# Chunk inverses by doubling: new partition halves for the middle product, masks on the product, and key scores and values inside the loop

## What is computed

```
def step(S, inp):
    r_t, w_t, k_t, v_t, kk_t, b_t = inp
    sa = einsum('bhvk,bhk->bhv', S, -kk_t)
    S = S * w_t[:, :, None, :] + sa[..., None] * b_t[:, :, None, :] + v_t[..., None] * k_t[:, :, None, :]
    return S, einsum('bhvk,bhk->bhv', S, r_t)
```

## Time and profile before

| | us |
|---|---|
| three runs | 2098.78, 2099.97, 2102.54 |
| median | 2099.97 |
| the profiled execution's own time | 2097.59 |
| its span, first to last instruction | 2095.7 |
| PE busy | 2038.5 (97% of the span) |
| DVE busy | 1278.4 (61%) |
| ACT busy | 890.4 (42%) |
| POOL busy | 131.5 (6%) |

### The profile page before, as it was taken

How to read it: one execution, slowest core, us unless ns; L and a number is a source line. 1 busy time by engine, 2 the same in 40 slices (tenths; PEclk the granted TensorE clock), 3 DMA queues, 4 the chain that set the end, 5 groups by cost and what they waited for, 6 DMA issues and landing times.

```text
span 2095.7 us, 32549 instructions
## 1 busy us (share of the span) xinstructions
PE 2038.5 (97%) x12860; PEld 1642.9 (78%) x12860; DVE 1278.4 (61%) x1564; ACT 890.4 (42%) x1219; POOL 131.5 (6%) x162
## 2 busy tenths in 40 slices
PE   7999999999999999999999999999999999999999
PEld 6689778878668888978878678877856888897887
DVE  7785465557765545665667655567865554566553
ACT  4432244434534434444545444434423444434442
POOL 2210100000010001000002011000000000000000
PEclk9999999999999999999999999999999999999999
DMA  8410165546247564555555258553312655555554
GB/s 298 128 63 4 42 201 186 182 160 203 99 152 210 185 205 161 171 193 188 165 186 191 74 168 226 187 191 124 115 54 92 202 187 181 170 172 181 183 172 147
DMA packets 92520, 335.31 MB, mean 160 GB/s; under 512 B 11150, under 2 KB 11284, under 8 KB 92095
## 3 DMA queue, kind: packets, MB, share of 16 engines
q1 hardware_dynamic: 85536, 311.62, 45.0%
q0 software_dynamic: 6880, 22.16, 3.7%
HBM read 332.69 MB, written 1.05 MB: 159 GB/s over the span
## 4 chain that ended last, share of the span: by engine, by line
PE 88%; DVE 7%; POOL 2%; issue 1%; ACT 1%; DMA 0%; DVEq 0%; SPq 0%; ACTq 0%; POOLq 0%
PE acc L327 40%; PE acc L404 20%; PE acc L380 10%; PE acc L829 2%; DVE w_lo L1431 2%; PE acc L577 2%; PE aux L577 1%; PE aux L750 1%; PE aux L960 1%; PE aux L953 1%; PE aux L785 1%; POOL rstd L2185 1%; POOL stat L2188 1%; PE aux L817 1%; PE aux L424 1%
## 5 line engine op out<-in xcount | busy, mean ns | idle before, releaser
L1431 DVE TENSOR_TENSOR w_lo<-w_raw,w_hi 128x1024 fp32r<-128x1024 f32 x588 | 716.3, 1225 | 590.3 <-ACT w_hi L1078 585.7
L1078 ACT ACTIVATE w_hi<-w_raw 128x1024 fp32r<-128x1024 f32 x588 | 620.3, 1059 | 805.0 <-PE acc L327 457.4
L327 PE MATMUL acc<-w_hi,operand_hi 128*128 128x512 f32 x1344 | 533.9, 397 | 26.3 <-DVE operand_lo L1586 11.9
L327 PE MATMUL acc<-w_hi,operand_lo 128*128 128x512 f32 x1344 | 525.0, 391 | 0.0
L327 PE MATMUL acc<-w_lo,operand_hi 128*128 128x512 f32 x1344 | 524.4, 390 | 0.0
L327 PEld LDWEIGHTS acc<-w_hi,operand_hi 128*128 128x128 f32 x1344 | 253.0, 188 | 87.5 <-DVE operand_lo L1452 15.0
L327 PEld LDWEIGHTS acc<-w_hi,operand_lo 128*128 128x128 f32 x1344 | 252.8, 188 | 53.8
L327 PEld LDWEIGHTS acc<-w_lo,operand_hi 128*128 128x128 f32 x1344 | 253.2, 188 | 50.5 <-issue 0.5
L404 PE MATMUL acc<-w_hi,hidden_hi 128*128 128x512 f32 x528 | 210.1, 398 | 0.0
L404 PE MATMUL acc<-w_hi,hidden_lo 128*128 128x512 f32 x528 | 208.5, 395 | 0.0
L404 PE MATMUL acc<-w_lo,hidden_hi 128*128 128x512 f32 x528 | 208.5, 395 | 0.0
(11 more groups left out here) (403 smaller groups left out, 2090.1 us busy)
## 6 DMA issues: line engine op xcount, KB each, us to landing
w_raw<-in_weights SPq DMA_DIRECT2D x588, 512.0 KB, 3.4
ln_gain<-in_gains POOLq DMA_DIRECT2D x7, 512.0 KB, 5.0
bias_at<-in_rpb POOLq DMA_DIRECT2D x12, 256.0 KB, 5.6
ln_gain<-in_ln_g POOLq DMA_DIRECT2D x4, 512.0 KB, 4.1
ln_bias<-in_ln_b POOLq DMA_DIRECT2D x4, 512.0 KB, 5.9
vec_rw<-in_vec POOLq DMA_DIRECT2D x3, 512.0 KB, 7.4
l_rw<-in_lora SPq DMA_DIRECT2D x1, 1152.0 KB, 10.6
iclr_rw<-in_xT SPq DMA_DIRECT2D x2, 512.0 KB, 4.5
```

Of the source, the lines that this page charges most:

```text
L327: mm = pe.matmul(acc[:, 2 * pair + t, :], (ah, al)[x][:, kt, t * P:(t + 1) * P], W[w][:, s, kk * 512:(kk + 1) * 512], start=(kt == 0 and ( ...
L1078: act.activation(whi[:, s, :], raw[:, s, :], ACT.Copy).then_inc(w_hi[s], 1)
L1431: dve.tensor_tensor(wlo[:, s, :], raw[:, s, :], whi[:, s, :].bitcast(F32), ALU.subtract).then_inc(w_lo[s], 1)
```

## The change

It edits six places; the diff below is cut where lines only repeat a pattern.

1. `LOWN` and all that makes it goes: 16 matmuls on PE, one DVE operation, two semaphores.
2. `by_own_rows` is called four times instead of twice, two of them with the column half swapped. The swapped copy goes to bank 6 and 7 and feeds `INV` directly from PSUM (`set_inverse`), so that `INV` holds its matrices on the other partition half from `INVT`.
3. `product` writes its result to the other half; `extension` reads `INV` and `TM` there and interleaves its two products kt by kt, so that four matmuls in a row use the four combinations of row and column half.
4. The mask moves from the extensions to the product: DVE now copies the product under the mask into a `TM` that holds the identity (`masked_product`), ACT copies the two extensions unmasked, and POOL puts the identity back into `TM` after each extension (16 copies of 128x512), having set it once before the loop (2 copies of 128x1024).
5. The four `by_both_rows` calls on `KTT` move into the loop, after g = 0, 1, 3 and 5, all on banks 6 and 7, each waiting for DVE's `set_keys` of the one before; the gates come after g = 7 and 9, and `keys_by_values` is interleaved with products 14, 15, 18 and 19.
6. DVE's order changes: `masked_product(0)` and `(1)` stand between the `set_turned` calls; the four splits come after `set_inverse(1)`; the wait for the gains is in `biased(0)`; the two `centred` calls stand ahead of `masked_product(14)`.

```diff
-            for n in range(len(STEPS) - 1):
-                for s in range(2):
-                    of = half_of(s)
-                    mm = pe.matmul(aux[of, 3, n * CH:(n + 1) * CH], LOWT[of, n, :], ident[of, of], start=True, stop=True, skip_group_check=True)
-            mm.then_inc(m["low_ready"], 1)
...
-            by_own_rows(6, 1)
+            by_own_rows(6, 0, swapped=1)
             pe.wait_ge(m["n_copied"], due(m["n_copied"], 2))
-            by_both_rows(0, 1, 0, BTT)
+            by_own_rows(0, 1)
             pe.wait_ge(m["rb_copied"], due(m["rb_copied"]))
-            by_both_rows(2, 1, 1, BTT)
+            by_both_rows(2, 1, 0, BTT)
             pe.wait_ge(m["rb_copied"], due(m["rb_copied"]))
-            by_both_rows(4, 0, 0, KTT)
...
+            by_both_rows(4, 1, 1, BTT)
+            pe.wait_ge(m["inv_set"], due(m["inv_set"], 2))
+            by_own_rows(6, 1, swapped=1)
...
+            def product(g, with_values=None):
+                u, b = g % UNITS, g % 2
+                for kt in range(KT):
+                    for s in range(2):
+                        of = half_of(s)
+                        mm = pe.matmul(ps(b)[half_of(1 - s), kt * CH:(kt + 1) * CH], NM[of, u // 2, u % 2, kt, :], INVT[of, u // 2, u % 2, kt, :],
+                                       start=(kt == 0), stop=(kt == KT - 1), skip_group_check=True)
+                    if with_values is not None:
+                        keys_by_values(with_values, kt)
+                mm.then_inc(m["t_ready"], 1)
...
             def extension(g):
...
+                if g == 0:
+                    pe.wait_ge(m["rb_copied"], due(m["rb_copied"], 2))
+                elif g >= 2:
+                    pe.wait_ge(m["e_copied"], due(m["e_copied"], 2 if g - 2 < last * UNITS else 1))
+                b = 2 + u if n == last else 2 + 2 * (g % 2)
+                for kt in range(KT):
+                    cols = slice(kt * CH, (kt + 1) * CH)
+                    for s in range(2):
+                        mm = pe.matmul(ps(b)[half_of(s), cols], INV[half_of(1 - s), t, e, kt, :], TM[half_of(1 - s), t, e, kt, :],
+                                       start=(kt == 0), stop=(kt == KT - 1), skip_group_check=True)
+                    if n < last:
+                        for s in range(2):
+                            mm = pe.matmul(ps(b + 1)[half_of(1 - s), cols], TM[half_of(1 - s), t, e, kt, :], INV[half_of(1 - s), t, e, kt, :],
+                                           start=(kt == 0), stop=(kt == KT - 1), skip_group_check=True)
+                mm.then_inc(m["e_ready"], 1)
+
+            def keys(k):
+                if k == 0:
+                    pe.wait_ge(m["inv_set"], due(m["inv_set"], 2))
                 else:
+                    pe.wait_ge(m["akrk_copied"], due(m["akrk_copied"]))
+                by_both_rows(6, k // 2, k % 2, KTT)
...
+            between = {0: lambda: keys(0), 1: lambda: keys(1), 3: lambda: keys(2), 5: lambda: keys(3), 7: lambda: gate(0), 9: lambda: gate(1)}
+            values_in = {14: 0, 15: 1, 18: 2, 19: 3}
...
# ACT, inside the loop
-                act.wait_ge(m["t_ready"], due(m["t_ready"]))
-                act.activation(TM[:, u // 2, u % 2], heads_of(4 + g % 2), ACT.Copy).then_inc(m["t_copied"], 1)
...
+                act.wait_ge(m["e_ready"], due(m["e_ready"]))
+                act.activation(INVT[:, t, e], heads_of(b), ACT.Copy).then_inc(m["e_copied"], 1)
+                if n < last:
+                    act.activation(INV[:, t, e], heads_of(b + 1), ACT.Copy).then_inc(m["e_copied"], 1)
+                if g in (14, 18):
+                    rhs((g - 14) // 4)
...
# DVE
+            def masked_product(g):
+                n, u = g // UNITS, g % UNITS
+                if g == 0 or g >= UNITS:
+                    dve.wait_ge(m["t_reset"], due(m["t_reset"], 1 if g else TT))
+                dve.wait_ge(m["t_ready"], due(m["t_ready"]))
+                dve.copy_predicated(TM[:, u // 2, u % 2], many(LOWT[:, n, :].bitcast(U32), KT), heads_of(g % 2)).then_inc(m["t_copied"], 1)
...
+            set_turned(1, 0, 2)
+            masked_product(0)
+            set_turned(1, 1, 4)
+            masked_product(1)
             set_inverse(1)
-            set_keys(0, 0, 4)
-            set_keys(0, 1, 6)
-            set_keys(1, 0, 0)
-            set_keys(1, 1, 2)
...
             ahead(q + 20, 4)
-            between = {0: lambda: bonus(0), 1: lambda: bonus(1), 2: lambda: biased(0), 3: lambda: biased(1), 4: lambda: gated(0),
-                       5: means, 6: lambda: centred(0), 7: lambda: centred(1), 9: lambda: gated(1)}
...
+            between = {2: lambda: set_keys(0), 3: lambda: set_keys(1), 4: lambda: bonus(0), 5: lambda: set_keys(2), 6: lambda: bonus(1),
+                       7: lambda: set_keys(3), 8: lambda: biased(0), 9: lambda: gated(0), 10: lambda: biased(1), 11: lambda: gated(1), 12: means}
+            for g in range(2, UNITS * len(STEPS)):
+                if g == 14:
+                    centred(0)
+                    centred(1)
+                masked_product(g)
                 if g in between:
                     between[g]()
...
# POOL
+            pool.wait_ge(m["rows_turned"], due(m["rows_turned"], 8))
+            for t in range(TT):
+                pool.tensor_copy(TM[:, t].rearrange("p e k n -> p (e k) n"), I64[:].unsqueeze(1).to_broadcast([P, HEADS, CH]))\
+                    .then_inc(m["t_reset"], 1)
             for k, name in enumerate(("gn_g", "gn_b")):
                 load(GN[:, k, :], A[name].partition_broadcast(P), m["gn_in"])
+            for g in range(UNITS * (len(STEPS) - 1)):
+                u = g % UNITS
+                pool.wait_ge(m["e_ready"], due(m["e_ready"]))
+                pool.tensor_copy(TM[:, u // 2, u % 2], I64[:].unsqueeze(1).to_broadcast([P, KT, CH])).then_inc(m["t_reset"], 1)
```

More of the change, by code:

```diff
@@ L530, in freed, with by_own_rows @@
                 pe.wait_ge(m["rows_copied_v"], due(m["rows_copied_v"]))
-            def by_own_rows(b, t):
+            def by_own_rows(b, t, swapped=0):
                 for kt, e, s in each():
                     of, at = half_of(e), chunk(t, s)
-                    mm = pe.matmul(ps(b + e)[half_of(s), kt * CH:(kt + 1) * CH], ART[of, 0, kt, at], BTT[of, kt, at], start=True, stop=True,
+                    mm = pe.matmul(ps(b + e)[half_of(s ^ swapped), kt * CH:(kt + 1) * CH], ART[of, 0, kt, at], BTT[of, kt, at], start=True, stop=True,
                                    skip_group_check=True)
@@ L611, in gate, with keys_by_values @@
                 mm.then_inc(m["gate_ready"], 1)
-            def keys_by_values(t):
-                if t == 0:
+            def keys_by_values(u, kt):
+                t, e = u // 2, u % 2
+                if u == 0 and kt == 0:
                     pe.wait_ge(m["gate_copied"], due(m["gate_copied"]))
                     pe.wait_ge(m["v_centred"], due(m["v_centred"]))
-                else:
+                elif u == 2 and kt == 0:
                     pe.wait_ge(m["rhs_copied"], due(m["rhs_copied"]))
-                for e in range(2):
-                    mm = by_chunks(2 * t + e, 6 + e, by_key(0), tokens(V))
-                mm.then_inc(m["av_ready"], 1)
-            between = {3: lambda: gate(0), 8: lambda: gate(1), 11: lambda: keys_by_values(0), 13: lambda: keys_by_values(1)}
-            pe.wait_ge(m["akrk_copied"], due(m["akrk_copied"]))
+                for s in range(2):
+                    of = half_of(s)
+                    mm = pe.matmul(ps(6 + e)[of, kt * CH:(kt + 1) * CH], AKRK[of, t, e, kt, 0, :], V[of, t, head(e, kt)],
+                                   start=(kt == 0), stop=(kt == KT - 1), skip_group_check=True)
+                if e and kt == KT - 1:
+                    mm.then_inc(m["av_ready"], 1)
+            between = {0: lambda: keys(0), 1: lambda: keys(1), 3: lambda: keys(2), 5: lambda: keys(3), 7: lambda: gate(0), 9: lambda: gate(1)}
+            values_in = {14: 0, 15: 1, 18: 2, 19: 3}
+            pe.wait_ge(m["n_copied"], due(m["n_copied"], 2))
             product(0)
@@ L629, in rwkv @@
                 if g + 2 < UNITS * len(STEPS):
-                    product(g + 2)
+                    product(g + 2, values_in.get(g + 2))
                 if g in between:
@@ L1676, in set_inverse, with set_keys @@
             def set_inverse(t):
+                dve.wait_ge(m["n_ready"], due(m["n_ready"], 2))
                 for e in range(2):
[L1679 to L1682 removed]
+                    dve.copy_predicated(INV[:, t, e], many(PICK[:, 2, :], KT), heads_of(6 + e)).then_inc(m["inv_set"], 1)
+            def set_keys(k):
+                t, x, b = k // 2, k % 2, 6
                 dve.wait_ge(m["akrk_ready"], due(m["akrk_ready"]))
```

63 lines of the change are left out of this document (14 added, 49 removed).

## The result

| | us |
|---|---|
| after, median of 20 runs (2099.37 to 2107.35) | 2105.02 |
| before, median of 20 runs beside them (2097.93 to 2105.06) | 2101.2 |
| ratio after to before | 1.0016, 95% interval 1.0009 to 1.0023 |
| after, the profiled execution's own time | 2105.97 |
| its span (before: 2095.7) | 2104.2 |

The change costs 0.16%, 3.4 us (1.9 to 4.8; the medians are 3.8 apart), where 0.8 us less was forecast. The two profiled executions are further apart, 8.5 us of span, so the first thing to learn is where those lie. Four marks do: the first score matmul, the first matmul behind the doubling, the first of the output projection, and the end. This is PE's timeline of after at the second and third mark, then of before at the third.

What follows compares the result with a forecast made beforehand. PE's doubling was taken as bound by instruction supply: 123.05 + 64.3 (packets) + 9.7 (waits, gates) = 197.1 instead of 198.46; with 0.8 more from packet phase, 2096.8 profiled, 2099.2 us against the median; range 2094 to 2105.5.

Steps and rivals of the forecast that it cites:

- The bound: Doubling after the change: PE limited by instruction supply, 256 per packet every 3.5 to 3.7 us, with stops put to issue.
- Rival 1: Doubling: no supply limit, products and extensions at array rate, 65.9 instead of 78.0 us, time 2088; chance 0.12.
- The halves: Extensions in the doubling: the two products run side by side on four array quarters, 64 matmul rows in 0.93 us.
- Rival 3: Extensions: the halves don't run side by side, doubling 79.9 to 84.6 us, time 2104; chance 0.05.
- The added waits: PE idle before keys(1), for set_keys(0), 2.8 us, and before the first values, for centred(1), some 3 us.
- POOL against DVE: Ahead of centred(1): one POOL copy colliding with DVE's SBUF work adds 0.6 us to DVE's chain.
- rival 2: Wait for centred(1) grows 3 us from POOL collisions, packets at 3.74 us add 3.4; time 2105; chance 0.13.
- The masks' removal: At 65.6 us: frees 0.6 us of PE but gains nothing, since the next matmul also waits for K's copy.
- First failed step: the packet: Doubling: 18.1 instruction packets remaining at 3.55 us each, 64.3 us in all.
- Second failed step: the overlap of the values' wait with its packet: Product 14, values waiting for centred(1): PE stands some 3 us, of which only 1.5 exceeds the packet's time.
- The keys' packet: Packet at the keys(1) wait for set_keys(0): PE idle 2.8 us, 1.9 beyond the packet's own time.
- the two gates: Packets holding a gate in the doubling: 6.4 us each, 2.85 over the usual packet, twice 5.7.

Runs made afterwards that it cites:

- run 2: Changed kernel with the two products of each extension one after the other instead of interleaved; 2106.34 us, ratio to before 1.0017.
- run 8: Kernel before with its gates' matmuls spread over steps 1 to 4 and 6 to 9; 2102.84 us, ratio to before 1.0001.
- run 4: Changed kernel with dummy matmuls in its two long waits and 62 of 64 key-score-by-value matmuls left out; 2100.41 us, ratio to before 0.9992.
- run 1: Changed kernel with three dummy 128x512 matmuls in each of its two long PE waits; 2099.97 us, ratio to before 0.9992.
- run 6: Changed kernel with serial extension products and dummy matmuls in its two long waits; 2105.69 us, ratio to before 1.0015.
- run 7: Changed kernel with each gate's four matmuls spread over four steps, DVE's order and the values moved to suit; 2100.17 us, ratio to before 0.9984.
- run 3: Changed kernel with 62 of 64 matmuls of key scores and values left out; 2103.49 us, ratio to before 1.0008.
- run 5: Changed kernel with DVE's work reordered so that neither long PE wait arises, weight splits late; 2103.26 us, ratio to before 1.0001.
- run 9: Changed kernel with gates spread and the two swapped own-row score calls replaced by four DMA copies; 2096.21 us, ratio to before 0.9973.

## Why the prediction was wrong, and where it was right

**The bound.** Right: the doubling of after is bound by instructions. Run 2 adds 15 us of array time for 1.3 us, run 8 shows that before has no such room, and the stops came as described. Rival 1 (no supply limit, 2088) is out by runs 2 and 4, and by the doubling of 82.0 instead of 65.9. The Trainium skill (page Runtime: NRT & Kernel Launch, section Instruction fetch mechanics) calls the crossing of a 256-instruction boundary mostly hidden; the stops of up to 1.41 us above, one per packet, disagree, and the measurement decides.

**The halves.** Right: 64 rows in 0.96 us. Rival 3 is out.

**The added waits.** Right in place and length: 2.8 and some 3 us were worked out, 3.1 and 3.1 measured (3.4 and 3.0 in the second profile). DVE's chain from gate(1) to `centred(1)` was put at 8.9 us and measured 8.6, from the end of the gate at about 172.5:

```profile
172.58 0.69 DVE L1754 TENSOR_TENSOR gain_gate<-aux,token_scratch 128x512 f32<-128x512 f32 x1 [3.38 <-PE aux L620]
...
175.60 2.27 DVE L1742 TENSOR_REDUCE stat<-v_rw 128x32 f32<-128x2048 f32 x1
...
178.75 2.34 DVE L1746 TENSOR_TENSOR v_rw<-v_rw,stat 128x1024 f32<-128x1024 f32 x2
```

**POOL against DVE.** The 0.6 us was not there, and rival 2 with it: the reduction took 2.27 as before, and the POOL copy beside it 0.62.

```profile
175.59 0.62 POOL L2273 COPY t_rw<-ident 128x512 f32<-128x512 f32 x1 [1.25 <-PE aux L603]
```

Rival 2's time, 2105, is what was measured, and half of its sum came true: it had packets at the upper end, 3.4 us more, and that is the first failed step below. The other half, 3 us from POOL beside DVE, did not come, so that the time fits is in part luck.

**The masks' removal** was put at nothing and is worth about 0.6 us by the first score matmul. That mark lies at 119.62 to 119.85 in the four profiles with the changed front part and no half clock near 106 us, at 120.20 and 120.43 in the two of before. Where the clock was at half for 3.4 us at about 108 it lies at 121.6 and 121.8, and for 6.8 us at about 106 at 123.3 to 123.7.

**First failed step: the packet.** "I take 3.55 us for one ... the quiet queue of the doubling is nearest the lower end." The doubling of after has 18 packets between 123.4 and 201.9 us. Fourteen of them hold neither a gate nor one of the two waits, and these are 3.3 to 4.1 us apart, 3.79 on the mean, the same in the second profile. That is 14 x 0.24 = 3.4 us on a term of 64.3. The prediction speaks of four steps; the stops of the earlier trace rows give three, 3.74, 3.73 and 3.47, all from one quiet stretch of one execution, and the choice within them was towards the low end; the quiet of the queue was no reason, since in after packets took 3.7 to 4.0 us with next to no other traffic (190 to 202 us).

**Second failed step: the overlap of the values' wait with its packet.** PE, the prediction says, "stands some 3 us, 1.5 over the packet": half of the wait was to be hidden in the packet's own time, 3.55 + 1.5 = 5.05 us. The packet took 7.2 in both profiles of after, 3.4 over the usual 3.79: all of the wait came on top, since no packet moved in it. With the next one it is 11.1 us (10.8 in the second profile), against 8.4 in run 1 and 8.5 in run 2, where one moved. Why it moves in one kernel and not in the other stays open. The clock is at its 1.2 GHz level from 179.9 to 190.1, and the text, which read PEclk 1.00 in before, never asked what new pauses would do to it; but the packet was overdue before the clock fell, and those that came under it were no longer than the rest, so the traces do not put the 2.1 us down to it. The keys' packet took 5.7 where 5.45 was counted, and the two gates 6.1 and 6.5 where 6.4 each was.

Added up: 76.7 predicted for the doubling, + 3.4 + 2.1 + 0.25 - 0.2 = 82.3, measured 82.0. The forecast's sign fell with these two terms. The first was an estimate of a size; the second took an overlap for granted that did not take place. Run 1 gives back 5 us by filling the waits, of which 2.6 are seen, in the second term; whether the packet or the clock makes the rest is not shown.

## What to carry to other kernels

Before making the array faster, count its instructions: where small fp32 matmuls come at 256 per 3.5 to 4 us, only fewer instructions, or array-heavy work spread between them, gains. When a change puts a pause into a stretch that the supply bounds, don't count the pause as hidden: look in the trace whether a packet moves in it. Filler matmuls in the pause are a cheap try, but say why they help only if something else is held fixed (5.0 us here, 0.6 with serial extensions). A half-clock stretch costs where the array is the bound and did not where the supply was. Take the price of a repeated unit from several executions, or carry its whole spread into the sum.

## What was not expected of the hardware

- The time between instruction packets is not the kernel's: means of 3.53 to 3.96 us in the 27 us behind the doubling over fourteen profiles, of kernels that issue nearly the same there. It may be the chip's: runs 4, 6, 7 and 8, all on one chip, have 3.87 to 3.96, and runs 1, 2, 3 and 5, all on another, 3.57 to 3.70. What sets it stays open.
- Whether an instruction packet moves while PE waits for another engine differs: none did in the second wait of both profiles of after and of run 3, in those of runs 1, 2, 4 and 6 one started within 0.9 us of its beginning.
- Weight traffic of 2.10 MB in 15 us went with stops of 2.0 us for instructions (run 5), longer than the at most 1.6 of the other profiles (but for run 9's 4.06, which went with a transfer's wait). That the one delays the other is inferred from their coincidence in one profile; it wasn't tried by itself.
- Half-clock stretches near 106, 545 and 805 us come and go between executions, those near 545 and 805 in the second profile of before too. One of 6.8 us near 106 goes with a first score matmul at 123.5 instead of 120. They explain part of the 7 us by which runs of the same kernel differ: over the 104 runs of before 0.001 of mean clock goes with some 1.9 us.
